# Experts of a mixture layer: f16 down products placed behind the next expert's first products, and the high parts of the down weights made by ScalarE

## The reference, cut to what matters

```
aff = softmax(x @ w_router)              # per token, over 16 experts
gates, idx = top_k(aff.T, cap)           # cap = 256 (prompt), 32 (sample)
xs = x[idx]
h  = silu(xs @ w_gate) * (xs @ w_up)     # 1024 -> 512
y  = (h @ w_down) * gates                # 512 -> 1024
out = zeros.at[idx].add(y); x = x + out
```

## Time and profile before

| | us |
|---|---|
| median of three runs | 2911.89 |
| lowest and highest | 2911.78, 2912.23 |
| span of the profiled execution | 2915.0 |
| TensorE busy in it | 2579.7 (88%) |
| VectorE, ScalarE, GpSimd busy | 1885.7 (65%), 1656.8 (57%), 1054.5 (36%) |
| mean granted TensorE clock | 0.946 |
| DMA | 415.99 MB, mean 143 GB/s |

### The profile page before, as it was taken

The page is one execution under the profiler, slowest core; times in us unless marked ns, Lnnn a source line. Parts: engine busy times, 40 slices in busy tenths (PEclk is TensorE's granted clock), DMA queues, the critical chain, the costliest instruction groups (busy, mean ns, idle before and its releaser), DMA issues. The chain is left out here.

```text
span 2915.0 us, 45718 instructions
## 1 busy us (share of the span) xinstructions
PE 2579.7 (88%) x16809; PEld 1446.8 (50%) x16809; DVE 1885.7 (65%) x2826; ACT 1656.8 (57%) x2708; POOL 1054.5 (36%) x984
## 2 busy tenths in 40 slices
PE   6899999859999999979898896999703999999998
PEld 4455555525555555553332232455402666666664
DVE  5456555548888888869888895544296455545542
ACT  6634444329999999978546655333241444444540
POOL 1221211138888888868008400222020212221221
PEclk9999999959999999999999997999956999999999
DMA  7423332325310111117877797445341667666762
GB/s 181 123 60 89 91 84 81 106 56 181 103 30 16 37 38 37 38 33 262 279 267 251 268 314 234 133 153 163 99 170 63 185 204 234 213 186 201 231 180 33
DMA packets 268924, 415.99 MB, mean 143 GB/s; under 512 B 55390, under 2 KB 148958, under 8 KB 267168
## 3 DMA queue, kind: packets, MB, share of 16 engines
q1 hardware_dynamic: 219696, 344.39, 36.7%
q0 software_dynamic: 10752, 37.75, 5.6%
q10 hardware_dynamic: 38288, 31.37, 3.8%
HBM read 280.56 MB, written 132.86 MB: 142 GB/s over the span
## 5 line engine op out<-in xcount | busy, mean ns | idle before, releaser
L1162 POOL TENSOR_TENSOR at_p<-at_pf,at_p 128x512 f16<-128x512 f32 x424 | 510.7, 1214 | 139.8 <-ACT at_p L1296 112.9
L1424 DVE TENSOR_REDUCE at_mxs<-at_pM 128x1 f32<-128x512 f32 x512 | 342.3, 684 | 74.6 <-PE at_pM L1323 63.0
L1295 ACT ACTIVATE at_pf<-at_pS,at_scale 128x512 f32<-128x512 f32 x520 | 358.3, 689 | 30.9 <-PE at_pS L1348 30.0
L1296 ACT ACTIVATE at_p<-at_pS,at_scale 128x512 f16<-128x512 f32 x520 | 355.4, 683 | 0.0
L1367 PEld LDWEIGHTS at_pO<-at_vv,at_p 128*128 128x128 f16 x4160 | 234.1, 98 | 141.0 <-POOL at_p L1162 31.9
L1367 PE MATMUL at_pO<-at_vv,at_p 128*128 128x129 f16 x4160 | 268.1, 207 | 8.3 <-POOL at_p L1162 6.5
L3062 PE MATMUL ex_pY<-mo_down,ex_hT 128*128 128x512 f32 x512 | 224.0, 595 | 0.0
L1323 PE MATMUL at_pM<-at_k,at_q 96*128 96x512 f16 x512 | 190.4, 391 | 28.7 <-DVE at_q L1410 18.4
L1346 PE MATMUL at_pS<-at_q,at_k 97*128 97x512 f16 (+1 forms) x528 | 200.2, 379 | 3.9 <-issue 2.2
L1347 PE MATMUL at_pS<-at_q,at_k 96*128 96x512 f16 (+1 forms) x528 | 200.0, 379 | 0.0
L1348 PE MATMUL at_pS<-at_q,at_k 96*128 96x512 f16 (+1 forms) x528 | 198.9, 377 | 0.0
(11 more groups left out here) (374 smaller groups left out, 5885.1 us busy)
## 6 DMA issues: line engine op xcount, KB each, us to landing
sp_rows<-s_F SPq DMA_DIRECT2D x76, 512.0 KB, 5.5
s_F<-fs_a SPq DMA_DIRECT2D x72, 512.0 KB, 3.1
mo_raw<-in_w_gate SPq DMA_DIRECT2D x32, 1024.0 KB, 7.4
mo_raw<-in_w_up SPq DMA_DIRECT2D x32, 1024.0 KB, 7.4
mo_down<-in_w_down SPq DMA_DIRECT2D x16, 2048.0 KB
s_G<-sp_gg SPq DMA_DIRECT2D x72, 256.0 KB, 4.2
sp_tab<-tab_spec SPq DMA_DIRECT2D x76, 224.0 KB, 4.0
s_QK<-pj_R ACTq DMA_DIRECT2D x18, 768.0 KB, 4.7
```

Of the source, the lines that this page charges most:

```text
L1162: eng.tensor_tensor(p2[r][:, :], pf[:, r, :], p1[r][:, :], ALU.subtract).then_inc(own_done if n in own else others_done, 1)
L1295: act.activation(pf[:, n % 4, :], pS[n % 2][:, 0:QB], ACT.Exp, scale=scale[:, 0:1])
L1296: act.activation(p1[n % 4][:, :], pS[n % 2][:, 0:QB], ACT.Exp, scale=scale[:, 0:1]).then_inc(pS_free, 1)
L1424: dve.tensor_reduce(mxs[:, j // NC, j % NC:j % NC + 1], pM[j % 2][:, :], AX.X, ALU.max).then_inc(pM_free, 1)
```

## The change

- The down product is done in f16. `h` gets a norm and is split into `hH` and `hL`, the down weights into `wdH` and `wdL`, and each f32 matmul becomes three f16 matmuls (hH*wdH, hH*wdL, hL*wdH).
- Two more norm chains are needed, one for `h` and one for the down weights: squares on ScalarE (`square_h`, `square_d`), a sum on TensorE (`add_h`, `add_d`), a move on ScalarE (`move_h`, `move_d`), two operations on GpSimd (`scale_h`, `scale_d`). ScalarE makes the high parts (`high_h`, `high_d`) and VectorE the low ones (`low_h`, `low_d`). `place` on VectorE forms one over the product of both scales and folds it into the gates.
- The down product of expert e moves into step e+1, behind product 10 and two turns. The turns go between the products and use only the two banks of `pT`; `xT` and `xL` get two buffers.
- The down weights have one f32 buffer, loaded in two parts of 1 MB once the low part before has been made. Gathers run two experts ahead. The squares of `square_part` go to a `junk` tile, each waiting for the one before it.

The core of the diff:

```diff
+            def square_h(e, f):
+                act.wait_ge(h_ready, FT * e + f + 1)
+                if f == 0 and not begins(e):
+                    act.wait_ge(h_summed, e)
+                elif f:
+                    act.wait_ge(h_squared, FT * e + f)
+                act.activation(h_junk[:, :], hT[:, f, :], ACT.Square, scale=1 / MOST, accum_out=h_sums[:, f:f + 1]
+                               ).then_inc(h_squared, 1)
+            def high_d(e, i):
+                if i == 0:
+                    act.wait_ge(d_powered, e + 1)
+                    if not begins(e):
+                        act.wait_ge(y_made, 2 * NC * e)
+                act.activation(down_part(wdH, i), down_part(wd, i), ACT.Copy, scale=d_scale[:, 0:1]).then_inc(dH_made, 1)
 # ScalarE, step(e, b, more)
+                gate(e, b, 0)
+                if not begins(e):
+                    move_h(e - 1)
+                    if more:
+                        move_size(act, weights, pN, e + 1)
+                    high_h(e - 1)
                 if more:
+                    make_hi(act, weights, e + 1, 1 - b, 0)
+                gate(e, b, 1)
+                if more:
+                    make_hi(act, weights, e + 1, 1 - b, 1)
+                    copies(e + 1, 1 - b, 0)
+                    copies(e + 1, 1 - b, 1)
+                    make_hi(act, weights, e + 1, 1 - b, 2)
+                    make_hi(act, weights, e + 1, 1 - b, 3)
+                for i in range(D_PARTS):
+                    square_d(e, i, more)
+                square_h(e, 0)
+                if more:
+                    copies(e + 1, 1 - b, 2)
+                    copies(e + 1, 1 - b, 3)
+                move_d(e)
+                square_h(e, 1)
+                gate(e, b, 2)
+                high_d(e, 0)
+                high_d(e, 1)
                 if more == 2:
+                    square_w(e + 2, 0)
+                square_h(e, 2)
+                if more:
+                    copies(e + 1, 1 - b, 4)
+                if more == 2:
+                    square_w(e + 2, 1)
+                gate(e, b, 3)
+                square_h(e, 3)
+                if more == 2:
+                    square_w(e + 2, 2)
+                    square_w(e + 2, 3)
 # TensorE
+            def down(e):
+                pe.wait_ge(dL_made, D_PARTS * e + D_PARTS)
+                pe.wait_ge(hL_made, e + 1)
+                pairs = ((hH, wdH), (hH, wdL), (hL, wdH))
...
+            def step(e, b, more):
...
+                product(e, b, 0, 0)
+                if not begins(e):
+                    if more:
+                        add_squares(pe, weights, pN, e + 1)
+                    add_h(e - 1)
+                product(e, b, 0, 1)
+                product(e, b, 1, 0, more)
+                if more:
+                    turn(e + 1, 1 - b, 0)
+                    turn(e + 1, 1 - b, 1)
+                if not begins(e):
+                    down(e - 1)
+                product(e, b, 1, 1)
+                if more:
+                    turn(e + 1, 1 - b, 2)
+                    turn(e + 1, 1 - b, 3)
+                add_d(e)
+                product(e, b, 2, 0)
+                product(e, b, 2, 1)
+                if more:
+                    turn(e + 1, 1 - b, 4)
+                product(e, b, 3, 0)
+                product(e, b, 3, 1)
...
             over_experts(pe, step)
+            add_h(E_N - 1)
+            down(E_N - 1)
 # VectorE, step(e, b, more), last = e - 1
+                if goes:
+                    low_h(last)
+                    place(last, other)
+                close(e, b, 0)
                 if more:
+                    find_back(e + 1, other)
+                    make_lo(dve, weights, e + 1, other, 0)
+                if goes:
+                    dve.wait_ge(placed, 2 * e)
+                    leave_sample(last, other)
+                    leave(last, other, 0, 0)
...
+                close(e, b, 1)
+                if more:
+                    leave_x(e + 1, other, 2)
+                    leave_x(e + 1, other, 3)
+                close(e, b, 2)
+                low_d(e, 0)
+                if more:
+                    leave_x(e + 1, other, 4)
+                close(e, b, 3)
+                low_d(e, 1)
 # GpSimd, step(e, b, more)
+                if not begins(e):
+                    scale_h(e - 1)
+                    if more:
+                        find_scale(pool, weights, e + 1, 1 - b)
                 if more == 2:
+                    gather(e + 2, b)
+                if not begins(e):
+                    scatter(e - 1, 1 - b, 2 - more)
+                scale_d(e)
```

More of the change, by code:

```diff
@@ L2950, in gather, with scatter @@
                                             ).then_inc(gathered[b], 16)
[L2952 to L2955, removed]
+            def scatter(e, b, left):
+                if not begins(e):
                     pool.wait_ge(scattered, 16 * NC * e)
@@ L2971, in _, with copies @@
         def _(act):
[L2972 to L2979, removed]
+            def copies(e, b, m):
+                act.wait_ge(x_turned, TURNS * e + m + 1)
+                if m == 0 and not early(e):
+                    act.wait_ge(up_made, FT * (e - 1))
+                for made, place in turned(b, m):
+                    last = act.activation(place(xT[b]), made, ACT.Copy, scale=x_scale[:, 0:1])
+                last.then_inc(xT_ready, 1)
             def gate(e, b, f):
@@ L2984, in gate @@
                     act.wait_ge(backed, e + 1)
[L2985 removed]
+                if not (begins(e) and f < 2):
                     act.wait_ge(h_ready, FT * e + f - 1)
                 act.activation(si[:, f % 2, :], pG[f % 2][:, 0:NTOK], ACT.Silu, scale=back[b][:, 0:1]).then_inc(silued, 1)
[L2989 to L3000 removed]
@@ L3002, in _, with turn @@
+            for m in range(TURNS):
+                copies(0, 0, m)
             over_experts(act, step)
+            move_h(E_N - 1)
+            high_h(E_N - 1)
         @block.tensor
         def _(pe):
[L3006 to L3014, removed]
+            def turn(e, b, m):
+                if m == 0:
+                    pe.wait_ge(gathered[b], 24 * e - 24 * b + 48)
+                if not (begins(e) and m < 2):
+                    pe.wait_ge(x_low, TURNS * e + m - 1)
+                out = pT[:, (b + m) % 2, :]
+                if m < PAIRS:
@@ L3026, in step @@
[L3026 to L3044, removed]
@@ new lines, in turn, with product @@
+                            last = pe.transpose(out[:, at:at + P], xs[b][c][:, k * P:(k + 1) * P], eye[:, :])
+                else:
+                    for k in range(SAMPLE_KD):
+                        last = pe.transpose(out[:, k * P:(k + 1) * P], xs[b][2][:, k * P:(k + 1) * P], eye[:, :])
+                last.then_inc(x_turned, 1)
+            def product(e, b, f, g, more=0):
+                out, done, free = ((pG, gate_made, silued), (pU, up_made, h_ready))[g]
+                if not (begins(e) and f < 2):
+                    pe.wait_ge(free, FT * e + f - 1)
+                if f == 1 and g and not begins(e):
+                    pe.wait_ge(y_ready, 2 * NC * (e - 1) + 2)
+                if f == 1 and not g and not begins(e):
+                    pe.wait_ge(h_sized, e)
+                    if more:
+                        pe.wait_ge(weights["sized"], e + 2)
+                if f == 3 and not g:
+                    pe.wait_ge(d_sized, e + 1)
+                if f == 0:
+                    pe.wait_ge(weights["lo_made"], W_PARTS * e + 2 * g + 2)
+                for k in range(KD):
+                    for w, x in ((hi, xT), (hi, xL), (lo, xT)):
+                        last = pe.matmul(out[f % 2][:, 0:NTOK], w[b][:, g, k, f * P:(f + 1) * P], x[b][:, k, :],
+                                         start=(k == 0 and w is hi and x is xT), stop=(k == KD - 1 and w is lo))
+                last.then_inc(done, 1)
@@ new lines, in add_h, with add_d @@
+            def add_h(e):
+                pe.wait_ge(h_squared, FT * e + FT)
+                if not begins(e):
+                    pe.wait_ge(h_sized, e)
+                pe.matmul(pH, weights["ones"][:, :], h_sums[:, :], start=True, stop=True).then_inc(h_summed, 1)
+            def add_d(e):
+                pe.wait_ge(d_squared, D_PARTS * e + D_PARTS)
+                if not begins(e):
+                    pe.wait_ge(d_sized, e)
+                pe.matmul(pD, weights["ones"][:, :], d_sums[:, :], start=True, stop=True).then_inc(d_summed, 1)
```

297 lines of the change are left out of this document (198 added, 99 removed).

## The result

The changed kernel takes 2925.7 us, the median of five runs (2922.92 to 2934.05), against 2912.23 for the kernel before in the same runs: a ratio of 1.0048, 95% interval 1.0036 to 1.0061. It is slower by about 13.5 us; 2926 and slower were forecast. The profiled execution has a span of 2932.2 us, 17.2 above that of before, and is the longest of the five. Executions of one kernel differ in where the granted clock of TensorE falls, ahead of the experts too: the trace of this execution has 322.8 us at half clock before the first product of expert 0, and that of experiment 5, the same kernel, 305.5.

The account below looks back on a forecast made before the run. TensorE, never waiting, was taken as the bound. Full-clock terms summed to -6.6 us; clock losses of 16 in the loop and 4.2 elsewhere made +13.6 on 2911.9, say 2926 us, range 2890 to 2942.

Parts of the forecast that it names:

- start: first turn to first product: Ahead of expert 0, five turns share two banks: 7.2 us instead of 5.73, +1.5.
- step 0, with its clock: First step, no down product but held by ScalarE: 32.5 us instead of 41.4, -8.9; its clock loss 1.7.
- loop at full clock: Steps 1 to 14 take 40.5 us each, 0.9 less than before: -12.6 us.
- clock in the loop: Two in three of the loop's gaps cost 1.7 us each: 1.1 per step, 16 us over 14 steps.
- step 15 and the end, with the clock: Last step carries the down product of 14, +12.0; h's open chain at the end +1.4; half speed there 2.5.
- What bounds the kernel: TensorE's chain of work sets the time; the f16 change cuts it from 41.4 to 37.7 us per expert.
- The stall: In steps 1 to 14 TensorE stands 2.7 us at `add_squares` for ScalarE's last squares; unhidden weight load adds 0.2.
- rival 2: ScalarE's stretch over a microsecond shorter: 14 x -1.1 more, 2894; without any stall about 2869; chance 0.24.
- Covers: In the loop, VectorE releases the last down-product bank 0.6 us before TensorE wants it; DMAs and GpSimd are hidden.
- the clock holds: First rival: the stall in the loop is there but costs no clock, 2909.5 us; chance 0.20.
- Rival 3: Each gap costs clock and ScalarE's small instructions cost 0.5 more: 14 x (0.6 + 0.5) more, 2941; chance 0.09.
- rival 4: Down products: f16 matmuls miss 0.216 us through their own weight loads, gaining under 3.6 us per expert; chance 0.01.

Follow-up runs that it names:

- experiment 5: The changed kernel run once more, unaltered, on another chip: ratio 1.0064 to the kernel before, median 2928.6 us.
- Experiment 7: Kernel of experiment 6, plus the small sums three slices into product 01 and VectorE's second low part behind a down-product release: ratio 0.9897, 2879.8 us.
- experiment 2: Changed kernel with `add_squares` and `add_h` behind product 01 instead of product 00, ScalarE's order untouched: ratio 0.9980, median 2907.6 us.
- experiment 6: Changed kernel with three squares of the gate and up weights earlier in ScalarE's order, nothing added or removed: ratio 0.9899, median 2881.8 us.
- experiment 3: Changed kernel with the first square of the gate and up weights moved ahead of the copies of turn 2: ratio 1.0045, median 2926.0 us.
- experiment 4: Changed kernel with the high parts of the down weights made by VectorE instead of ScalarE: ratio 1.0057, median 2929.0 us.
- experiment 1: Changed kernel with 20 unused matmuls of 128x288 ahead of `add_squares` in steps 1 to 14: ratio 1.0018, median 2918.6 us.
- Experiment 9: Kernel of experiment 8, with ScalarE squaring the down weights right behind silu 0 in step 0 alone: ratio 0.9861, median 2872.4 us.
- experiment 8: Kernel of experiment 7, plus 42 unused matmuls at the very end, 10 behind the last product and 32 behind the last `add_h`: ratio 0.9881, 2878.4 us.

## Why the prediction was right

The total was right, and so were its mechanism and the sign of every term. Three sizes were off by 2.6 to 3.7 us and partly cancel. Each term as forecast, and as the two traces show it:

| term | forecast | measured |
|---|---|---|
| start: first turn to first product | +1.5 | +1.65 (7.38 for 5.73) |
| step 0, with its clock | -7.2 | -3.5 (37.91 for 41.42) |
| loop at full clock | -12.6 (40.5 a step) | -10.0 (40.68) |
| clock in the loop | +16 | +12.8 |
| step 15 and the end, with the clock | +15.9 | +16.6 (69.0 for 52.4) |

With the start 0.3 us earlier the measured column makes the 17.2 us between the two spans; the forecast column makes 13.6. The medians differ by 13.5. That this is the forecast to 0.1 us is luck: executions of the changed kernel differ by 11 us, and the terms measured in the traces add up to 3.6 us more than forecast.

- **What bounds the kernel.** Right: the f16 products are worth 3.55 us per expert once nothing else is late, where 3.7 was forecast. Experiment 7 went from 41.41 to 37.86 us a step. The terms shown for TensorE's work (41.4 - 3.58 - 0.46 + 0.24) make 37.6, not the 37.7 written, and 40.5 for the step follows from 37.6. Measured are 37.86 and 2.82 for stall and sum (2.9 forecast), which make the 40.68; over 14 steps this is the 2.6 us by which the loop missed.
- **The stall.** Right in place, cause and size: 2.55 us idle and a longer small sum, where 2.7 and 0.2 were forecast. Experiments 2 and 6 remove it by order alone. The prediction read the whole stretch from product 20 as its cause. That is the first of two limits only 0.3 us apart (steps of 40.68 and 40.36); the second, the two squares behind h3, was not in it, and experiments 3 and 4 show it. So rival 2 was priced wrongly: a stretch shorter by a microsecond would have taken 0.3 us from the wait, and not 1.1.
- **The clock.** The loss was right in kind: in the trace of experiment 1, filling the gaps gives 12.9 us back. The share was too high, since 5 of 14 gaps struck and not two in three, and the price too low, since three of the five cost 3.17 us and not 1.7. The two errors partly cancel, at 16 for 12.8. Waits of 2.55 us in this kernel and of 2.23 us in experiments 3 and 4 came with falls; with the two small sums and their weight loads TensorE was without large matmuls for about 3.0 us in the one and 2.7 in the other. The rule that the prediction quotes from the Trainium skill, TensorE: Matmul & The Clock Gate, section "Why this matters for your kernels", no gaps above about 3 us, is thus no limit below which a gap costs nothing here.
- **Step 0.** The term that was missized most, by 3.7 us. The order of ScalarE was laid out rightly (waits of 1.72 and 4.56 us, where 1.9 and 4.7 were forecast), but only 1.7 us was set for the clock. Product 00 took 5.33 us and product 20, behind the second wait, 5.65, where 2.94 had been set for each. The clock came up 4.9 us after the first product began, where it had been up before it in the kernel before, and it was down again behind the wait at `add_d`, for some 10 us (both stretches of the changed kernel, columns of rows 2):

```profile
2243.00:2247.80 4.80, 4.80 (x21) 3.02 (x22) 0.23 (x2) 1.28 (x1) 3.04 (x4) 0.50 0.46 135
2261.60:2271.70 10.10, 5.93 (x26) 3.89 (x27) 5.26 (x5) 6.17 (x13) 0.77 (x2) 0.50 0.83 292
```

Experiment 9 takes away the wait, and most of the half clock behind it. That step 0 then takes 32.5 us, the figure of the prediction, is chance: that figure was laid out for ScalarE's old order with both waits at full clock, and in experiment 9 one wait is gone and 8.9 us (5.5 at the start, 3.4 later) are at half clock.
- **Covers.** VectorE made TensorE wait nowhere in the loop of the changed kernel. In one step it released the last bank of the down products at 2551.15, 0.8 us before TensorE used it (2551.96), where 0.6 was forecast. In experiment 2, where the down products come sooner in the step, TensorE waits for VectorE 0.4 us at a time on average. DMAs, GpSimd and the weight loads of the f16 products cost nothing.
- **The rivals.** That the clock holds (2909.5) and that ScalarE is quicker than laid out (2894) are excluded by the trace; VectorE or a DMA as the bound likewise. Rival 3's longer small instructions are not there (14.45 us for the stretch laid out at 14.46), nor rival 4: the 48 long down products take 10.37 us, where 10.35 was forecast.

## What to carry to other kernels

When work is moved to an engine with room on average, lay its written order along the bound engine's for one whole step, from the last thing that it must wait for to the first result that the bound engine asks for: here 14.5 us of work stood where 12 fitted, while the same engine was idle for some 5 us earlier in the step (3.7 ahead of the copies of turn 2, 1.7 ahead of silu 2). Find all instructions that could stand in those idle times, and recheck after each move, since a second limit may stand 0.3 us behind the first. A stall that returns every step is to be priced with the clock that it may cost, and the trace of the same kernel with its stalls filled by unused matmuls measures that price.

## What was not expected of the hardware

- A wait of constant length, 2.55 us every 40.7 us, does not cost the clock constantly, but in a regular pattern: the steps of the changed kernel were 40.68 three times, 43.85, 42.33, 40.68 three times, 43.85, 42.33 and so on. A shorter wait (2.23 us every 40.36) had more falls, seven in 14 steps. Whether a gap costs thus does not follow from its length alone, and a little less stall need not save any of the clock's part.
- The prediction's share of two in three leaned on four gaps of one execution, and one execution was too few. The code ahead of the experts is the same in all eleven traces, and so are these gaps: the one of 1.8 us came with a fall in 3 of the 11, 1.89 in 7, 2.52 in all 11, and 2.77 in one. The gap of 1.8 us in experiment 5, and that of 2.77 us in the changed kernel's trace (both held in rows 9):

```profile
86.00:92.00 6.00, 3.97 (x19) 2.10 (x18) 3.24 (x5) 4.03 (x9) 2.22 (x2) 0.80 0.01 4
558.00:566.00 8.00, 5.23 (x23) 2.53 (x22) 2.90 (x5) 2.21 (x4) 0.00 (x0) 0.79 0.01 2
```

- The kernel before differs by up to 8 us between runs on one chip (2909.7 to 2917.5), so the gains of experiments 7, 8 and 9 over the ones before them show in the traces and not in the medians.
- `tensor_scalar` from f32 to f16 took 1.28 us for 2048 elements on VectorE, ScalarE's copy 1.9 and VectorE's `scalar_tensor_tensor` of that size 2.35.
